# Relative position bias: the table's high and low halves multiplied in one pass of 64 stationary columns and added after the read-back

## The chip, the cores and the metric

The kernel runs on one core of one Trainium2 chip. The metric is the device time of one execution in microseconds (us), as the median of several executions. TensorE is the matrix engine (PE in the rows, PEld for its weight loads), VectorE is DVE, ScalarE is ACT, GpSimd is POOL and SyncE is SP. ACTq and SPq are the instruction queues of ACT and SP where they issue DMAs.

## The reference

Two transformer blocks over 256 rows of width 2048, in float32. The first has retention, a block attention and a feed-forward layer. The second has a memory attention (C), a sparse attention with a learned index (A) and a latent attention (B), then gates and an output product. Only attention A reads the part that is changed, the relative position bias:

```python
def t5_bucket(dist):                       # 32 buckets
    n = jnp.maximum(dist, 0)
    large = 16 + (jnp.log(max(n,1) / 16) / math.log(128 / 16) * 16).astype(int32)
    return jnp.where(n < 16, n, jnp.minimum(large, 31))

# in dsa_attention, for a block of 128 queries:
score = einsum('bths,bth->bts', relu(q_idx . k_idx), w_idx) * IDX_SCALE   # causal
sel   = top_k(score, 64)
logits = (q . k[sel]) * A_SCALE
bias   = rel_table[t5_bucket(pos_q - pos[sel])]       # rel_table is (32, 8 heads)
p      = softmax(where(valid, logits + bias, -inf))
```

So for each of 8 heads, 256 queries and up to 256 keys, one entry of a 32 by 8 table is added to a logit.

## The kernel before, in words

**The stream.** All weights lie in memory as 842 groups of 128 partitions by 1024 floats (512 KB), in the order of use. SP loads one group at a time into a ring of four buffers (RAW). ACT copies a group to WH, rounded to the matrix engine's float32 form (the high half, L931). DVE writes WL = RAW - WH (the low half, L1379). TensorE takes the group in 12 matmuls of 512 columns (L600 to L602: high by high, high by low, low by high). The ring ties them: the load of group g+4 waits for DVE's split of group g, and ACT's split of group g+4 waits until TensorE has used group g. A product of 512 output columns is 8 groups. Each engine runs its own program in a fixed order written out by hand; between the splits, at fixed steps p of a phase, it does the small work of the attentions.

**The bias, first part (phase gates_ret, 32 groups).** At six steps of each of two loop turns (BIAS_AT), 12 times in all: POOL writes distances DI for 8 queries of each of the four groups of 32 partitions, against 128 keys (L506); DVE turns them into a one-hot OH, 128 partitions (4 query groups by 32 buckets) by 1024 columns (L1556, L1557); TensorE multiplies with the table (L744). REL holds the table as a high and a low half, each 128 by 32 (8 heads for each of the four query groups, block by block). For each of two PSUM banks it runs two passes that sum in the same 32 output rows: high half times one-hot, low half times one-hot. ACT copies the 32 rows to BE (L1105) and stores them to bias_scratch in memory (L1107), where a row is a pair of query group and head.

**The bias, second part.** After phase a_proj ACT issues four DMAs (L1252) that read bias_scratch back with queries on the partitions, one DMA for each 32 partitions, into BIAS (128 by 8 heads by 384). They stand in ACT's program behind the last evacuation of a_proj and ahead of everything of phase b_proj. DVE waits for them at step 3 of gates_b0 (L1779) and adds the selection mask to BIAS in two halves (L1781). The heads of attention A read BIAS at L1424.

**Phase b_proj (24 groups)**, which follows the four issues, holds the index scores. At step 0 TensorE transposes the index keys (L869) and ACT copies them (L1261). At odd steps TensorE transposes one pair of index heads (L874) and ACT copies it to QKT (L1264), behind its split of that step. At even steps from 2 on TensorE multiplies them (L882, L883), behind a wait for ACT's copy (idx_ready), and ACT applies the relu (L1269, L1270). DVE sums at odd steps (L1755), and selects from step 18 on.

Of the kernel before, what the change touches and what calls it, by code (L numbers as in the profile page):

```python
# [21 lines left out]
F32 = mybir.dt.float32  # L22
F32R = mybir.dt.float32r
I32 = mybir.dt.int32
ALU = mybir.AluOpType
ACT = mybir.ActivationFunctionType
# [3 lines left out]
P = 128  # L30
# [19 lines left out]
CAUS = 3 * P  # L50
BUCKETS, REL_HEADS = 32, 8
# [106 lines left out]
class Chain:  # L158
# [5 lines left out]
    def link(self, ins):  # L164

        self.k += 1
        ins.then_inc(self.sem, 1)
        self.wait(self.sem, self.total + self.k + self.i * self.per if self.per else self.total + self.k)
# [9 lines left out]
def build(nc, x_in, mem_in, w_stream, params, final_w, pos_pack, constants, out):  # L178
    with ExitStack() as ctx:
        def sem(name):  # L180
            return ctx.enter_context(nc.semaphore(name))
# [5 lines left out]
        def take(nbytes):  # L187
            at = cursor[0]
            cursor[0] += nbytes
            return at  # L190

        def sb(name, shape, dt, at):
            return nc.alloc_sbuf_tensor_at(name, shape, dt, offset=at)

        KB = 1024
        at_x, at_ht, at_pa, at_pb, at_u2 = take(16 * KB), take(32 * KB), take(36 * KB), take(16 * KB), take(16 * KB)
        at_u0, at_u1 = take(16 * KB), take(16 * KB)
# [24 lines left out]
        CKV = sb("CKV", [P, T, 2 * W], F32, at_sgx)  # L222
        JUNK = sb("JUNK", [P, T, D], F32, at_u1)
        BIAS = sb("BIAS", [P, REL_HEADS, CAUS], F32, at_u2)
        LATT = sb("LATT", [P, 6, 2, S], F32R, at_sgx + 4 * KB)

        SG = {"merge_moba": sb("SG_MOBA", [P, T, CH], F32, at_u2), "merge_c": sb("SG_C", [P, T, CH], F32, at_u2 + 12 * KB),
# [14 lines left out]

        DI = sb("DI", [P, 8, P], I32, at_x)
        OH = sb("OH", [P, 2, 8, P], F32R, at_x + 4 * KB)
        BE = sb("BE", [32, 8, P], F32, at_x + 12 * KB)
        RAW = sb("RAW", [P, RING, GK, CH], F32, take(16 * KB))
        WH = sb("WH", [P, RING, GK, CH], F32R, take(16 * KB))
        WL = sb("WL", [P, RING, GK, CH], F32R, take(16 * KB))
# [5 lines left out]
        REL = sb("REL", [P, 2, 32], F32R, take(256))  # L254
# [7 lines left out]
        assert cursor[0] <= nc.sbuf_usable_end  # L262
        PS = ctx.enter_context(nc.psum_tensor("PS", [P, 8, 512], F32))

        bias_scratch = nc.dram_tensor("bias_scratch", (32, 3, 32, P), F32, kind="Internal").ap()
        x_scratch = nc.dram_tensor("x_scratch", (S, D), F32, kind="Internal").ap()

        def con(name, rows=P):
# [72 lines left out]
        bias_copied = sem("bias_copied")  # L341
        bias_stored = sem("bias_stored")
        bias_loaded = sem("bias_loaded")
# [240 lines left out]
        def _(pe):  # L584
# [151 lines left out]
            def bias_step(i, p):  # L736
                if p not in BIAS_AT:
                    return
                k = At(BIAS_AT.index(p), i, len(BIAS_AT))
                pe.wait_ge(onehot, k.count(1))  # L740
                pe.wait_ge(bias_copied, k.count(1))
                for b in range(2):
                    for part in range(2):
                        ins = pe.matmul(PS[0:32, 4 + b, :], REL[:, part, :],  # L744
                                        OH[:, k.base % 2, 4 * b:4 * b + 4, :].rearrange("p q s -> p (q s)"), start=part == 0, stop=part == 1)
                ins.then_inc(bias_done, 1)
            pe.wait_ge(rel_lo, 1)
            product_loop("gates_ret", 2, [(GD, HT)] * 2, bias_step)
# [92 lines left out]
            with pe.Fori(0, FB - 1) as b:  # L841
                g = At(g0 + 2 * GD, b, 3 * GD)
# [59 lines left out]
            for c in range(3):  # L902
                product(At(g0), At(n0 + c), 2 * c, 2, LATT)
            for c in range(4):
                product(At(g0), At(n0 + 3 + c), 6 + c, 1, LATT[:, 4:6])

# [15 lines left out]
        def _(act):  # L922
            ch = Chain(act.wait_ge, act_chain)
            link = ch.link
# [100 lines left out]
            for t in range(T):  # L1025
                act.wait_ge(x_first[t], 16)
                ins = act.activation(PS[:, 4 * t:4 * t + 4, :].rearrange("p b n -> p (b n)"), X[:, t, :], ACT.Square,
                                     scale=D ** -0.5, accum_out=MS[:, t:t + 1])
# [9 lines left out]
            g = At(GROUP0["moba_proj"])  # L1038
# [10 lines left out]
            for a in range(2):  # L1049
                act.activation(ROPE[:, 1, a], ANG[:, 0], ACT.Sin)  # L1050
                ins = act.activation(ROPE[:, 0, a], ANG[:, 1], ACT.Sin, scale=-1.0, bias=con("hpi"))
# [46 lines left out]
            def bias_step(i, p):  # L1098
                if p not in BIAS_AT:
                    return  # L1100
                s = BIAS_AT.index(p)
                k = At(s, i, len(BIAS_AT))
                act.wait_ge(bias_done, k.count(3))
                act.wait_ge(bias_stored, k.count(1) * 16)
                act.activation(BE[:].rearrange("p (b q) s -> p b (q s)", b=2), PS[0:32, 4:6, :], ACT.Copy).then_inc(bias_copied, 1)  # L1105
                act.wait_ge(bias_copied, k.count(2))
                act.dma_start(bias_scratch[:, s % 3, ds(i * 16 + s // 3 * 8, 8), :], BE[:]).then_inc(bias_stored, 16)  # L1107

# [5 lines left out]
            for p in range(NCH * GW):  # L1114
# [7 lines left out]
                if p == 3:  # L1122
                    act.wait_ge(mem_loaded, 16)
                    for t in range(T):
                        ins = act.activation(JUNK[:, t, :], MEMR[:, t, :], ACT.Square, scale=D ** -0.5, accum_out=MS[:, t:t + 1])
# [21 lines left out]
            for p in range(GD):  # L1147
                g = At(GROUP0["mem0"])
# [37 lines left out]
            with act.Fori(0, FB - 1) as b:  # L1186
                g = At(g0 + 2 * GD, b, 3 * GD)
# [9 lines left out]
            for p in range(GD):  # L1197
                g = At(GROUP0["mem1"])
# [8 lines left out]
            for p in range(2 * GD):  # L1207
                g = At(GROUP0["mem2"])
# [4 lines left out]
                if p in (4, 5):  # L1213
                    act.wait_ge(x_done, p - 2)
                    ins = act.activation(PS[:, 4:8, :].rearrange("p b n -> p (b n)"), X[:, p - 4, :], ACT.Square,
                                         scale=D ** -0.5, accum_out=MST[:, 0, 0, p - 4:p - 3])
# [20 lines left out]
            with act.Fori(0, 4) as i:  # L1237
                ch.enter(i, 3)
                g = At(GROUP0["a_proj"], i, 2 * GD)
                for p in range(2 * GD):  # L1240
                    split(g, p + RING)
                    if p % GD == GD - 1:
                        c = p // GD
                        dst = PAC[:, ds(i * 2 + c, 1)].rearrange("p a t n -> p (a t) n")
# [3 lines left out]

            act.wait_ge(head_out, C0 + 4 + 1)
            act.wait_ge(bias_stored, 16 * (NBIAS + 1))  # L1250
            for g in range(4):
                act.dma_start(BIAS[32 * g:32 * g + 32, :, :].rearrange("p h (s k) -> p h s k", s=3),  # L1252
                              bias_scratch[8 * g:8 * g + 8].rearrange("h s p k -> p h s k")).then_inc(bias_loaded, 16)

            squares = [(PAC[:, h // 4, t, h % 4 * P:(h % 4 + 1) * P], MST[:, 0, t, h:h + 1]) for h in range(8) for t in range(T)]
            squares += [(PAC[:, 2, t, h * P:(h + 1) * P], MST[:, 1, t, h:h + 1]) for h in range(2) for t in range(T)]
# [20 lines left out]
            for p in range(3 * GD):  # L1277
                g = At(GROUP0["b_proj"])
# [13 lines left out]
            def latent_squares(p):  # L1292
# [11 lines left out]
                elif 4 <= p < 7:  # L1304
                    transposed("lat", LATT, [2 * p - 8, 2 * p - 7], "lat")
            gates_b("gates_b0", 0, 1, latent_squares)
# [64 lines left out]
        def _(dve):  # L1371
            ch = Chain(dve.wait_ge, dve_chain)
            link = ch.link
# [41 lines left out]
            def head_scores(br, H, M, h):  # L1415
# [6 lines left out]
                if br["causal"]:  # L1422
                    mask = BIAS[:, ds(h, 1), :].rearrange("p a n -> p (a n)") if br is ASP else con("mask")
                    link(dve.scalar_tensor_tensor(out=SC[:, 0:CAUS], in0=PS[:, 6, 0:CAUS], scalar=br["scale"], in1=mask,  # L1424
# [155 lines left out]
            for p in range(NCH * GW):  # L1580
# [4 lines left out]
                if p in (8, 12):  # L1585
                    dve.wait_ge(norm_rstd, 2)
                    ins = scaled_rows(MEMR, MEMR, p // 4 - 2)
# [82 lines left out]
            with dve.Fori(0, FB - 1) as b:  # L1670
                ch.enter(b, 2 * 2 * FT)
                g = At(g0 + 2 * GD, b, 3 * GD)
# [74 lines left out]
            for p in range(3 * GD):  # L1747
                split(At(GROUP0["b_proj"]), p + RING)
                if p % 2 and 3 <= p < TOPK_AT:
                    k = (p - 3) // 2  # L1750
                    dve.wait_ge(idx_relu, k + 2)
                    for j, src in enumerate((SC, PR)):
                        for t, cols in halves:
                            w = PAC[:, 7, t, IW + 2 * k + j:IW + 2 * k + j + 1]
                            ins = dve.scalar_tensor_tensor(out=PT[:, cols], in0=src[:, cols], scalar=w, in1=PT[:, cols],  # L1755
                                                           op0=ALU.mult, op1=ALU.add)
                        link(ins)
                    dve.sem_inc(idx_sum, 1)
                if p >= TOPK_AT:
                    topk_round(p - TOPK_AT)  # L1760
            for p in range(GD):
                split(At(GROUP0["gates_b0"]), p + RING)
                if p < 2:
                    topk_round(3 * GD - TOPK_AT + p)
                if p == 2:

                    link(dve.tensor_scalar(left[:, 0:CAUS], left[:, 0:CAUS], TAKEN, -1.0, ALU.is_equal, ALU.add))
                    link(dve.scalar_tensor_tensor(out=SC[:, 0:CAUS], in0=left[:, 0:CAUS], scalar=-NEG, in1=con("mask"),
                                                  op0=ALU.mult, op1=ALU.add))

                    dve.wait_ge(lat_rstd, 1)
                    for t in range(T):
                        dve.tensor_scalar(PB[:, t, 0:512], PB[:, t, 0:512], MS[:, t:t + 1], None, ALU.mult)
                        dve.tensor_scalar(PB[:, t, PB_KV], PAC[:, 7, t, KV_LAT], MS[:, 2 + t:3 + t], None, ALU.mult)
                    dve.tensor_copy(PB[:, :, PB_KPE], PAC[:, 7, :, KPE]).then_inc(lat_rows, 1)
                if 4 <= p < 7:
                    transposed("lat", LATT, [2 * p - 8, 2 * p - 7], "lat")
                if p in (3, 4):
                    dve.wait_ge(bias_loaded, 64)  # L1779
                    half = BIAS[:, (p - 3) * 4:(p - 2) * 4]  # L1780
                    dve.tensor_tensor(half, half, SC[:, 0:CAUS].unsqueeze(1).broadcast_to([P, REL_HEADS // 2, CAUS]),  # L1781
                                      ALU.add).then_inc(sel_ready, 1)
# [166 lines left out]
```

## Time and profile before

| | before |
|---|---|
| median of 3 runs | 2513.46 us (2513.05, 2513.46, 2515.88) |
| span of the profiled execution | 2513.8 us |
| PE busy | 2480.8 us, 99% |
| DVE busy | 1502.5 us, 60% |
| ACT busy | 1232.3 us, 49% |
| POOL busy | 233.7 us, 9% |
| mean granted TensorE clock | 0.998 |
| DMA | 461.07 MB, 130129 packets |

The page gives the profiled execution's span and no further time of it; the median of the runs lies 0.34 us under that span. Busy times of matmuls overlap: a matmul of 512 columns is written with 0.39 us, while the next one starts 0.23 us after it. What one costs is the distance between two starts.

### The profile page before, as it was taken

Reading aid. Unit: us, or ns where it says so; the run is one execution under the profiler, and the core shown is the slowest. Engines: PE = TensorE matmul, PEld = TensorE weight load, DVE = VectorE, ACT = ScalarE, POOL = GpSimd, SP = SyncE. Lnnn points to the kernel's source line nnn. Section 1 sums busy time; section 2 is a strip of 40 time slices with the busy share of each in tenths; the row PEclk is TensorE's granted clock in tenths of the full one; section 3 lists DMA queues with packets and bytes.
Section 4 is the critical chain, followed back from the end, with each engine's and each line's share of the span. In section 5 each row is a group of like instructions: output and inputs, shape, how many; then the busy total and the mean of one; then the engine's idle time right before and its main releaser. Section 6 shows DMA issues by size and latency. Waiting matters only on the chain.

```text
span 2513.8 us, 35958 instructions
## 1 busy us (share of the span) xinstructions
PE 2480.8 (99%) x11882; PEld 2054.1 (82%) x11882; DVE 1502.5 (60%) x1799; ACT 1232.3 (49%) x1632; POOL 233.7 (9%) x277
## 2 busy tenths in 40 slices
PE   7999999999999999999999999999999999999999
PEld 6888878877888888888888888888877788777887
DVE  4444445486656777777777776444446655554564
ACT  4444545544445444444444445454547555555443
POOL 0011224231000000000000000010100100432000
PEclk9999999999999999999999999999999999999999
DMA  6555545565655555555555556555564545444654
GB/s 235 192 186 169 173 162 171 171 216 194 210 185 176 187 188 190 186 188 188 189 187 190 186 189 211 194 186 171 170 193 160 173 156 183 164 152 149 226 184 159
DMA packets 130129, 461.07 MB, mean 183 GB/s; under 512 B 14224, under 2 KB 17552, under 8 KB 129168
## 3 DMA queue, kind: packets, MB, share of 16 engines
q1 hardware_dynamic: 121536, 443.60, 52.9%
q10 hardware_dynamic: 8528, 16.58, 2.0%
q8 instruction: 43, 0.70, 0.1%
q14 instruction: 22, 0.18, 0.0%
HBM read 454.36 MB, written 5.77 MB: 183 GB/s over the span
## 4 chain that ended last, share of the span: by engine, by line
PE 95%; DVE 1%; POOL 1%; ACT 1%; issue 1%; DMA 0%; ACTq 0%; POOLq 0%; SPq 0%; DVEq 0%
PE PS L600 20%; PE PS L602 20%; PE PS L601 20%; PE PS L800 13%; PE PS L802 7%; PE PS L824 3%; PE PS L826 3%; PE PS L825 3%; PE PS L681 1%; PE PS L698 1%; PE PS L661 1%; PE PS L641 1%; DVE WL L1379 1%; ACT WH L931 0%; PE PS L744 0%
## 5 line engine op out<-in xcount | busy, mean ns | idle before, releaser
L1379 DVE TENSOR_TENSOR WL<-RAW,WH 128x1024 fp32r<-128x1024 f32 x842 | 1056.2, 1256 | 952.8 <-ACT WH L931 948.3
L931 ACT ACTIVATE WH<-RAW 128x1024 fp32r<-128x1024 f32 x842 | 890.4, 1060 | 1158.6 <-PE PS L602 764.3
L600 PE MATMUL PS<-WH,HT 128*128 128x512 f32 x1824 | 730.4, 400 | 3.0 <-DVE HT L1408 1.2
L602 PE MATMUL PS<-WH,HT 128*128 128x512 f32 x1824 | 712.9, 391 | 0.0
L601 PE MATMUL PS<-WL,HT 128*128 128x512 f32 x1824 | 711.7, 390 | 0.0
L800 PE MATMUL PS<-HT,WH 128*128 128x512 f32 x1408 | 498.2, 399 | 0.0
L600 PEld LDWEIGHTS PS<-WH,HT 128*128 128x128 f32 x1824 | 343.4, 188 | 78.7 <-issue 9.1
L602 PEld LDWEIGHTS PS<-WH,HT 128*128 128x128 f32 x1824 | 343.0, 188 | 73.8
L601 PEld LDWEIGHTS PS<-WL,HT 128*128 128x128 f32 x1824 | 343.7, 188 | 67.3
L802 PE MATMUL PS<-HT,WL 128*128 128x256 f32 x1408 | 395.4, 281 | 0.0
L800 PEld LDWEIGHTS PS<-HT,WH 128*128 128x128 f32 x1408 | 264.6, 188 | 65.7
L802 PEld LDWEIGHTS PS<-HT,WL 128*128 128x128 f32 x1408 | 266.0, 189 | 0.4
L824 PE MATMUL PS<-WH,ACTT 128*128 128x512 f32 x352 | 137.2, 390 | 0.0
L826 PE MATMUL PS<-WH,ACTT 128*128 128x512 f32 x352 | 137.1, 389 | 0.0
L825 PE MATMUL PS<-WL,ACTT 128*128 128x512 f32 x352 | 137.0, 389 | 0.0
L600 PE MATMUL PS<-WH,U 128*128 128x512 f32 x320 | 130.3, 407 | 2.1 <-issue 2.1
L602 PE MATMUL PS<-WH,U 128*128 128x512 f32 x320 | 125.8, 393 | 0.0
L601 PE MATMUL PS<-WL,U 128*128 128x512 f32 x320 | 125.5, 392 | 0.0
L437 POOL TENSOR_TENSOR MS<-MS,CONST 128x2 f32<-128x2 f32 (+1 forms) x8 | 1.6, 198 | 1073.1 <-ACT PS L963 785.1
L826 PEld LDWEIGHTS PS<-WH,ACTT 128*128 128x128 f32 x352 | 66.1, 188 | 14.1
L824 PEld LDWEIGHTS PS<-WH,ACTT 128*128 128x128 f32 x352 | 66.1, 188 | 13.8
L825 PEld LDWEIGHTS PS<-WL,ACTT 128*128 128x128 f32 x352 | 66.1, 188 | 13.5
(235 smaller groups left out, 1915.1 us busy)
## 6 DMA issues: line engine op xcount, KB each, us to landing
RAW<-w_stream SPq DMA_DIRECT2D x842, 512.0 KB, 3.3
X<-x_in SPq DMA_DIRECT2D x2, 1024.0 KB, 6.7
MEMR<-mem_in ACTq DMA_DIRECT2D x1, 2048.0 KB, 11.5
X<-x_in ACTq DMA_DIRECT2D x4, 512.0 KB, 4.2
x_scratch<-X ACTq DMA_DIRECT2D x4, 512.0 KB, 3.8
X<-x_scratch ACTq DMA_DIRECT2D x1, 2048.0 KB, 9.8
out<-X ACTq DMA_DIRECT2D x4, 512.0 KB, 3.5
bias_scratch<-BE ACTq DMA_DIRECT2D x12, 128.0 KB, 2.5
```

The costliest lines, as they stand in the source:

```text
L600: pe.matmul(o, hi, WH[:, slot, kk, :], start=k == 0, stop=False)
L601: pe.matmul(o, hi, WL[:, slot, kk, :], start=False, stop=False)
L602: ins = pe.matmul(o, lo, WH[:, slot, kk, :], start=False, stop=k == nq * GK - 1)
L641: ins = pe.transpose(PS[:, 4 + at % 4, t * P:(t + 1) * P], src[:, t, k * P:(k + 1) * P], ident)
L661: ins = pe.transpose(PS[0:n, 4 + a, c * S + t * P:c * S + (t + 1) * P], QK[:, a, t, c * P:c * P + n], ident)
L800: pe.matmul(PS[:, half + f, :], WH[:, slot, kk, f * P:(f + 1) * P], HT[:, k, :, :], start=k == 0, stop=False, skip_group_check=True)
L802: ins = pe.matmul(PS[:, half + f, 0:S], WL[:, slot, kk, f * P:(f + 1) * P], HT[:, k, 0, :], start=False, stop=k == KT - 1, skip_group_chec ...
L824: pe.matmul(o, hi, WH[:, slot, kk, :], start=k == 0, stop=False)
L825: pe.matmul(o, hi, WL[:, slot, kk, :], start=False, stop=False)
L826: ins = pe.matmul(o, lo, WH[:, slot, kk, :], start=False, stop=k == FT - 1)
L931: act.activation(WH[:, g.slot(j)], RAW[:, g.slot(j)], ACT.Copy).then_inc(hi_split, 1)
L1379: dve.tensor_tensor(WL[:, s], RAW[:, s], WH[:, s].bitcast(F32), ALU.subtract).then_inc(lo_split, 1)
```

## The change

REL is taken as 64 stationary columns (32 of the high half, 32 of the low half), so one pass for each bank gives 64 output rows: the high products and the low products apart. BE, its copy and its store have 64 rows, and bias_scratch has 64. Eight DMAs in place of four read it back, four into BIAS and four into BIASL, and DVE adds the two in halves at steps 10 and 12 of b_proj. The wait for the loads moves from gates_b0 to there.

```diff
+        BIASL = sb("BIASL", [P, REL_HEADS, CAUS], F32, at_u1)
-        BE = sb("BE", [32, 8, P], F32, at_x + 12 * KB)
+        BE = sb("BE", [64, 8, P], F32, at_x + 12 * KB)
-        bias_scratch = nc.dram_tensor("bias_scratch", (32, 3, 32, P), F32, kind="Internal").ap()
+        bias_scratch = nc.dram_tensor("bias_scratch", (64, 3, 32, P), F32, kind="Internal").ap()
...
                 for b in range(2):
-                    for part in range(2):
-                        ins = pe.matmul(PS[0:32, 4 + b, :], REL[:, part, :],
-                                        OH[:, k.base % 2, 4 * b:4 * b + 4, :].rearrange("p q s -> p (q s)"), start=part == 0, stop=part == 1)
+                    ins = pe.matmul(PS[0:64, 4 + b, :], REL[:].rearrange("p a n -> p (a n)"),
+                                    OH[:, k.base % 2, 4 * b:4 * b + 4, :].rearrange("p q s -> p (q s)"), start=True, stop=True)
                 ins.then_inc(bias_done, 1)
...
-                act.activation(BE[:].rearrange("p (b q) s -> p b (q s)", b=2), PS[0:32, 4:6, :], ACT.Copy).then_inc(bias_copied, 1)
+                act.activation(BE[:].rearrange("p (b q) s -> p b (q s)", b=2), PS[0:64, 4:6, :], ACT.Copy).then_inc(bias_copied, 1)
...
             act.wait_ge(bias_stored, 16 * (NBIAS + 1))
-            for g in range(4):
-                act.dma_start(BIAS[32 * g:32 * g + 32, :, :].rearrange("p h (s k) -> p h s k", s=3),
-                              bias_scratch[8 * g:8 * g + 8].rearrange("h s p k -> p h s k")).then_inc(bias_loaded, 16)
+            for part, dst in enumerate((BIAS, BIASL)):
+                for g in range(4):
+                    h = 32 * part + 8 * g
+                    act.dma_start(dst[32 * g:32 * g + 32, :, :].rearrange("p h (s k) -> p h s k", s=3),
+                                  bias_scratch[h:h + 8].rearrange("h s p k -> p h s k")).then_inc(bias_loaded, 16)
...
+                if p in (10, 12):
+                    dve.wait_ge(bias_loaded, 128)
+                    half = slice((p - 10) * 2, (p - 10) * 2 + 4)
+                    link(dve.tensor_tensor(BIAS[:, half], BIAS[:, half], BIASL[:, half], ALU.add))
...
                 if p in (3, 4):
-                    dve.wait_ge(bias_loaded, 64)
```

## Rows read from the trace of the kernel before

**Rows 1.** The page: busy time of each engine, chain that ended last.
```profile
PE 2480.8 (99%) x11882; PEld 2054.1 (82%) x11882; DVE 1502.5 (60%) x1799; ACT 1232.3 (49%) x1632; POOL 233.7 (9%) x277
...
PE 95%; DVE 1%; POOL 1%; ACT 1%; issue 1%; DMA 0%; ACTq 0%; POOLq 0%; SPq 0%; DVEq 0%
```

**Rows 2.** Timeline of PE, first bias step: start, length, engine, line, tiles.
```profile
508.79 1.08 PE L744 MATMUL PS<-OH,REL 128*32 128x512 f32 x4
509.71 0.40 PE L600 MATMUL PS<-WH,HT 128*128 128x512 f32 x1
509.94 0.39 PE L601 MATMUL PS<-WL,HT 128*128 128x512 f32 x1
```

**Rows 3.** Instructions of L744 and tile BE: min/median/max ns, first and last start.
```profile
L744 PEld LDWEIGHTS PS<-OH,REL x48: 106/108/109, 508.6 to 598.5; 128*32 128x32 f32 x48
...
L1105 ACT ACTIVATE BE<-PS x12: 995/1016/1019, 510.0 to 600.1; 32x1024 f32<-32x1024 f32 x12
```

**Rows 4.** Timeline of ACT and its queue, end of a_proj and start of b_proj.
```profile
1858.96 0.93 ACTq L1252 DMA_DIRECT2D BIAS<-bias_scratch  x2
...
1859.92 2.79 ACTq L1252 DMA_DIRECT2D BIAS<-bias_scratch  x2
1862.84 1.06 ACT L931 ACTIVATE WH<-RAW 128x1024 fp32r<-128x1024 f32 x1 [2.21 <-issue]
1863.80 0.36 ACT L1261 ACTIVATE QKT<-PS 128x256 f32<-128x256 f32 x1
1864.99 1.06 ACT L931 ACTIVATE WH<-RAW 128x1024 fp32r<-128x1024 f32 x1 [0.82 <-PE PS L602]
1865.96 0.36 ACT L1264 ACTIVATE QKT<-PS 128x256 f32<-128x256 f32 x1
```

**Rows 5.** L1252, issues 3 and 4 one by one, with time to landing.
```profile
L1252 ACTq DMA_DIRECT2D BIAS<-bias_scratch x1: 1044/1044/1044, 1859.9 to 1859.9; - x1
...
DMA to landing us min/median/max: 9.4/9.4/9.4
...
L1252 ACTq DMA_DIRECT2D BIAS<-bias_scratch x1: 1720/1720/1720, 1861.0 to 1861.0; - x1
...
DMA to landing us min/median/max: 11.8/11.8/11.8
```

**Rows 6.** DMA queues (q1 SP, q10 ACT), stretches 1857:1861, 1861:1865, 1865:1869: packets, MB, share.
```profile
q1 hardware_dynamic: 227, 0.80, 55.2%
q10 hardware_dynamic: 109, 0.06, 4.8%
...
q10 hardware_dynamic: 1713, 0.86, 105.3%
q1 hardware_dynamic: 1, 0.00, 0.4%
...
q10 hardware_dynamic: 773, 0.39, 55.6%
```

**Rows 7.** Timeline of PE around the first product of index scores, b_proj step 2.
```profile
1867.47 0.39 PE L602 MATMUL PS<-WH,HT 128*128 128x512 f32 x1
1867.79 0.50 PE L882 MATMUL PS<-QKT 64*128 64x128 f32 x4
```

**Rows 8.** Timeline of DVE, split of step 15 of b_proj; below it L1781.
```profile
1913.59 1.23 DVE L1379 TENSOR_TENSOR WL<-RAW,WH 128x1024 fp32r<-128x1024 f32 x1 [2.60 <-ACT WH L931]
...
L1781 DVE TENSOR_TENSOR BIAS<-BIAS,SC x2: 1749/1750/1751, 1952.6 to 1956.2; 128x1536 f32<-128x1536 f32 x2
```

**Rows 9.** PE after its first long wait (timeline); stretch 18:21 by windows (third from last: clock).
```profile
14.28 1.94 PE L641 MATMUL PS<-CONST,ROWS 128*128 128x128 f32 x8 [14.28 <-DVE ROWS L1391]
17.43 0.79 PE L600 MATMUL PS<-WH,HT 128*128 128x512 f32 x1 [1.21 <-DVE HT L1408]
...
21.34 0.40 PE L600 MATMUL PS<-WH,HT 128*128 128x512 f32 x1
...
18.00:21.00 3.00, 3.00 (x8) 2.31 (x7) 3.00 (x4) 1.56 (x2) 0.00 (x0) 1.00 0.57 198
```

## The prediction

> **What bounds the kernel now.** I read the page first. PE is busy for 99% of the span and carries 95% of the chain that ended last; DVE and ACT stand at 60% and 49% [rows 1]. So an instruction taken off PE is worth its full distance to the next one, and a microsecond that PE has to wait costs a microsecond. Work put on DVE, ACT or a queue costs nothing until it makes PE wait. Hence I went to the two places that the change touches and read there how late the thing is that PE waits for: the timeline of PE at a bias step [rows 2], and the timelines of ACT, its queue and PE at the start of b_proj, where the read-back is issued [rows 4, 7], with the packets of the DMA queues beside them [rows 6].
>
> **Removed: 24 matmuls.** In a bias step four matmuls of 512 columns take 508.79 to 509.71 us, 0.92 us, or 0.23 us each, the same as the 0.23 us between two matmuls of the weight stream with 128 stationary columns, at 509.71 and 509.94 [rows 2]. Since 32 and 128 columns cost the same, 64 will. The load of the columns takes 0.108 us for 32 [rows 3] and fits under the 0.23 us. There are 48 such matmuls [rows 3]; 24 go: 24 x 0.23 = 5.5 us off PE, with nothing behind them that was late. It can't be more by much, and not less unless 64 columns were slower than 128.
>
> **Copy and store.** The copy takes 1.016 us on 32 partitions [rows 3]; ACT's split of 1024 elements on 128 partitions takes 1.06 us [rows 4], so 64 rows add nothing. The store is 256 KB in place of 128 KB. Nothing needs it before the next bias step's copy; ACT has only the wait for it there. Bounds: 0 to a us or two of waiting for ACT, which a ring of four groups hides. I take 0.
>
> **The four further issues.** This is the cost, and I work it out in full, because the issues stand in ACT's program in front of its splits and copies of b_proj. The four issues before took 0.93 us for two and 2.79 us for two; ACT stood still 2.21 us for them and went on at 1862.84, 0.13 us after the last issue ended at 1862.71 [rows 4]. The third took 1.044 us and the fourth 1.720 [rows 5], so they grow: half of 0.93, 1.04, 1.72. That is not the price of an instruction but of a queue that fills. One DMA is 384 KB in runs of 512 bytes, 768 packets. The third issue ended near 1860.96, with 2304 packets issued and at most 109 moved [rows 5, 6]: 2200 pending. The fourth ended at 1862.71; 109 + 1.71 us x 428 a us (1713 in 4 us) = 841 moved of 3072 [rows 6]: 2230 pending. Both agree: an issue ends when some 2200 packets are left pending. Eight DMAs are 6144 packets, so the eighth issue ends when 3944 have moved. By 1865, 1822 have. From 1865 to 1869 the stream's loads share the engines: 773 was measured [rows 6], with two loads there; with one load of 128 packets (1.24 us of the engines, by the 227 packets that held 55.2% of them for 4 us [rows 6]) it is up to (4 - 1.24) x 428 = 1180. I take the middle, 980. That leaves 1144 packets, 2.7 us alone: **the last issue ends near 1871.7, 9.0 us later than before.**
>
> What waits behind it: ACT's split, its copy of the keys, the next split, its copy L1264. Before, these ran with a pause of 0.82 us for PE [rows 4]; back to back they end 2.8 us after the last issue, and with a hand-over of 0.2 us TensorE's L882 can start 3.0 us after it. It started at 1867.79, straight behind its matmul of 1867.47 [rows 7], so before there was 2.1 us of slack. After: 1871.7 + 3.0 = 1874.7, which is **6.9 us of PE standing idle**. The rest of the ring is no later: the groups of steps 1 to 3 are split already, and step 4's split is done before PE gets there.
>
> **After a stand-still the matmuls are slow for a while.** At the start of the kernel, after 14.28 us without matmuls, eight transposes and 1.21 us more of waiting, the products start at 17.43, and the tenth at 21.34 [rows 9]: nine distances in 3.9 us, where nine of 0.23 are 2.1 us. That is 1.8 us lost. The granted clock is written 1.00 there, the 2.4 GHz level, though the mean distance of 0.43 us is nearly twice the usual; I go by the distance. The other waits of PE are far shorter than 7 us, so the trace shows only what 14 us does. Bounds 0 to 1.8 us; I take 1.8, because nothing at all would run on PE for 6.9 us.
>
> The Trainium skill, "TensorE: Matmul & The Clock Gate", Part 1, says that the throttled state is the default and activity releases it; after an idle gap matmuls start at the half rate again. The start of this trace agrees. By that rule the 1.8 us is due here too; without it the sum is 1.8 us lower.
>
> **Weight loads.** A stream load issued in the BIAS traffic moved one packet in 4 us [rows 6]. In the changed kernel the traffic lasts longer, but ACT's own stand-still also holds back the next loads (they wait for the splits), and when they start about 1100 packets of BIAS are left, as before, where PE started L882 straight behind the stream [rows 7]. I take 0; bound up to 2 us.
>
> **The two additions.** 128 x 1536 on DVE: L1781 of the same size takes 1.75 us [rows 8]. Behind the split of an even step DVE stands idle for 2.60 us, as until 1913.59 [rows 8]; the addition fits. The fourth load landed 11.8 us after its issue [rows 5], so the eighth lands by some 1871.7 + 12 = 1884. Steps 2 to 15 lie between 1867.79 and 1913.59 [rows 7, 8], 3.5 us each, so step 10 comes near 1896, and the stall shifts it further: the wait is met. The wait removed at gates_b0 was long met. 0 us; if the cover were gone, two times 1.75 us of DVE, inside a ring four groups deep.
>
> **Sum:** -5.5 + 6.9 + 1.8 = +3.2 us. On the profiled span 2513.8 that is 2517.0; on the median, 0.34 us under the span, 2516.7. What tells from no change in this kernel is about 0.2%, 5.0 us; this is 0.13%.
>
> **Rivals.**
> (a) *The issues stay short and PE never waits.* Four times the mean of the first two, 0.47 us [rows 4], are 1.9 us, within the 2.1 us of slack (1867.79 - 1862.71 - 3.0). Then 2513.46 - 5.5 = 2508.0, faster by 0.22%. Against it: the fourth issue took 1.72 us [rows 5], over three times that.
> The Trainium skill, "DMA: Bandwidth & Descriptors", section "Issuing engines are not separate DMA queues", says the sequencer's time to initiate a DMA is usually small beside the DMA itself. By it (a) holds. The rows disagree for this access pattern: 1.72 us for the fourth.
> (b) *The growth stops at 1.72 us.* Four times 1.72 is 6.9 us of delay, the stall 4.8 us, no slow matmuls: 2513.46 - 5.5 + 4.8 = 2512.8, not slower. For it: only four points of the growth are seen.
> (c) *Slower: each further issue lasts as long as landings are apart at the end.* Issue 3 landed at 1869.3 and issue 4 at 1872.8, 3.5 us apart [rows 5]. Then the delay is 14.0 us, the stall 11.9 us, plus 1.8: 2513.46 - 5.5 + 11.9 + 1.8 = 2521.7, slower by 0.33%. It holds if the mixed rate of 773 packets in 4 us [rows 6] persists although the stream pauses; it is over 0.2% slower from a delay of some 11 us on.
> (d) *The passes aren't halved in time* (64 columns cost two passes): then +5.5 on my sum, 2522.2. The 128-column rows at 0.23 us speak against it; 2 in 100.
>
> **How the numbers follow.** My forecast 0.52 (own range 2514.3 to 2519), (a) 0.13, (b) 0.13, (c) and (d) 0.22. Faster by over 0.2% is (a) less what misses the bound: 0.12. Slower by over 0.2% (above 2518.5) is (c), (d) and the top of my own case: 0.27. The rest 0.61. The range runs from (a) at 2508.0 to just under (c), 2521.0.
>
> **What would show it.** L744: 24 matmuls, 0.46 us from the first to the next L600. L1252: eight issues, the last ending 8 to 10 us later against the first than before, and ACT's idle time "issue" near 11 us. PE: a wait of about 7 us before L882 at step 2 of b_proj, released by ACT's L1264, and spacings of 0.43 us behind it. DVE: two additions of 1.8 us without a wait. Wrong if PE has no such wait, if it is over 10 us, or if PE waits elsewhere in b_proj for late weights.

## The result: 6.6 us slower

| | before | after |
|---|---|---|
| median of 7 runs | 2515.88 us | 2522.48 us |
| lowest to highest | 2513.05 to 2516.61 | 2520.21 to 2524.24 |
| span of the profiled execution | 2513.8 us | 2520.3 us |
| mean granted clock | 0.998 | 0.997 |

The ratio of the runs is 1.0027, 95% interval 1.0018 to 1.0037: slower, and clear of no change. I had forecast +3.2 us on 2513.46 and a range up to 2521.0. The measured time lies outside it, partly because the kernel before itself came out 2.4 us higher over seven runs than over the first three: two of the first three lay at 2513, and the other five of the seven between 2515.66 and 2516.61. The 0.34 us of which I made a rule (the median of the runs lies under the span) compared two different executions. The device time of the kernel before is 1.74 to 1.94 us over the span of the same execution wherever both are listed, so the profiled execution, with its span of 2513.8, is one of the higher group, and 2513.46 is a median of the lower one. For the changed kernel the distance is about 2.2 us. The difference of the spans, 6.5 us, is what the profiles explain. One of the eleven executions of before_late_copy_wait (below) took 3539.27 us at a mean granted clock of 0.656; it is counted in the median given there, 2512.88, which is 2512.62 without it. Line numbers of the changed kernel differ a little (L600 to L602 became L601 to L603, L1252 became L1254).

**Bias stage.** The timeline of PE in the changed kernel, the first bias step, the seventh and the twelfth (answers to [rows 2]) with the wait behind it, then the instructions of L744 and of the copy and store of BE (to [rows 3]):

```profile
508.93 0.62 PE L744 MATMUL PS<-OH,REL 128*64 128x512 f32 x2
...
555.97 0.67 PE L744 MATMUL PS<-OH,REL 128*64 128x512 f32 x2 [0.19 <-DVE OH L1559]
...
594.27 0.63 PE L744 MATMUL PS<-OH,REL 128*64 128x512 f32 x2
597.44 0.47 PE L601 MATMUL PS<-WH,U 128*128 128x512 f32 x1 [2.54 <-issue]
```
```profile
L744 PEld LDWEIGHTS PS<-OH,REL x24: 132/134/137, 508.8 to 594.3; 128*64 128x64 f32 x24
...
L1105 ACT ACTIVATE BE<-PS x12: 997/1003/1011, 510.1 to 596.3; 64x1024 f32<-64x1024 f32 x12
...
L1107 ACTq DMA_DIRECT2D bias_scratch<-BE x12: 481/482/571, 511.3 to 597.5; - x12
```

Half the matmuls are gone, as forecast. From the first to the twelfth start of L744 it was 89.29 us (508.79 to 598.08) and is 85.34: 3.95 us less, where eleven times 0.46 would be 5.06. New is PE waiting for the one-hot (L1559). Behind the twelfth step PE waits at the end of the stage, 2.54 us here. In the kernel before it did so too, 2.07 us, which I had not read. The rows name no releaser; before_late_copy_wait, below, shows that it is the wait for the last copy of BE:

```profile
601.24 0.56 PE L600 MATMUL PS<-WH,U 128*128 128x512 f32 x1 [2.07 <-issue]
```

**Start of b_proj.** The timeline of ACT and its queue in the changed kernel (answers to [rows 4]), then the single issues 5 to 8 into BIASL (to [rows 5]):

```profile
1855.15 0.93 ACTq L1254 DMA_DIRECT2D BIAS<-bias_scratch  x2
1855.81 1.01 ACT L936 ACTIVATE PAC<-PS 128x1024 f32 x1
1856.12 2.74 ACTq L1254 DMA_DIRECT2D BIAS<-bias_scratch  x2
1858.88 10.47 ACTq L1254 DMA_DIRECT2D BIASL<-bias_scratch  x4
1869.48 1.06 ACT L931 ACTIVATE WH<-RAW 128x1024 fp32r<-128x1024 f32 x1 [12.66 <-issue]
...
1871.65 0.38 ACT L1266 ACTIVATE QKT<-PS 128x256 f32<-128x256 f32 x1
```
```profile
L1254 ACTq DMA_DIRECT2D BIASL<-bias_scratch x1: 1743/1743/1743, 1858.9 to 1858.9; - x1
...
L1254 ACTq DMA_DIRECT2D BIASL<-bias_scratch x1: 2614/2614/2614, 1860.7 to 1860.7; - x1
...
L1254 ACTq DMA_DIRECT2D BIASL<-bias_scratch x1: 4192/4192/4192, 1863.3 to 1863.3; - x1
...
L1254 ACTq DMA_DIRECT2D BIASL<-bias_scratch x1: 1836/1836/1836, 1867.5 to 1867.5; - x1
```

The issues grow to 4.19 us; the eighth takes 1.84. ACT stands still for 12.66 us in place of 2.21. PE in the same place (answers to [rows 7]), then PE's granted clock by windows (columns: stretch, length, busy time of PE, PEld, DVE, ACT, POOL, granted clock, DMA share, GB/s):

```profile
1863.68 0.39 PE L603 MATMUL PS<-WH,HT 128*128 128x512 f32 x1
1872.08 0.81 PE L882 MATMUL PS<-QKT 64*128 64x128 f32 x4 [8.01 <-ACT QKT L1266]
...
1874.26 0.63 PE L602 MATMUL PS<-WL,HT 128*128 128x512 f32 x1
1874.68 0.63 PE L603 MATMUL PS<-WH,HT 128*128 128x512 f32 x1
```
```profile
1866.00:1868.00 2.00, 0.00 (x0) 0.00 (x0) 0.00 (x0) 0.00 (x0) 0.00 (x0) 1.00 1.21 188
1868.00:1870.00 2.00, 0.00 (x0) 0.00 (x0) 0.00 (x0) 0.52 (x1) 0.00 (x0) 0.60 1.22 212
1870.00:1872.00 2.00, 0.00 (x0) 0.00 (x0) 1.34 (x2) 2.00 (x5) 0.00 (x0) 0.50 1.21 211
1872.00:1874.00 2.00, 1.92 (x9) 1.27 (x10) 2.00 (x2) 1.18 (x3) 0.00 (x0) 0.50 1.28 220
...
1875.00:1877.00 2.00, 2.00 (x9) 1.57 (x9) 0.00 (x0) 0.00 (x0) 0.00 (x0) 0.95 1.03 339
```

PE waits 8.01 us for ACT's copy; in the middle of the wait the granted clock falls to 0.50, 1.2 GHz, and it stays there for the first 2 to 3 us of work, with 0.42 us between matmuls. Of the forecast's steps this is the one that was right in kind, place and releaser.

**Where the 6.5 us are,** by the starts of the same instructions in both kernels:

| stretch | shift after it | change (+ is slower) |
|---|---|---|
| up to the first L744 (508.79, 508.93) | +0.1 | +0.1 |
| first to twelfth L744 | -3.8 | -3.9 |
| twelfth L744 to first matmul of up_ret (601.24, 597.44) | -3.8 | 0.0 |
| up to L882 at step 2 of b_proj (1867.79, 1872.08) | +4.3 | +8.1 |
| L882 at step 2 to step 4 (1874.58, 1880.31), slow matmuls | +5.7 | +1.4 |
| gates_b0, behind a PE wait of 2.48 us | +6.7 | +0.9 |

The fourth and fifth lines are the stall, 9.5 us in all. The last line was not in my sum, and the second was there with another size. All of it is of one profiled execution of each kernel.

### The profile page after: what moved, and what is told of

It reads as the page before. It is cut to its first block, busy times and chain, and to the rows that moved or that the text cites. A ratio compares the mean times of both kernels' runs of the same rounds, so it can differ in the third digit from the quotient of the medians.

```text
span 2520.3 us, 35918 instructions
## 1 busy us (share of the span) xinstructions
PE 2479.1 (98%) x11858; PEld 2054.2 (82%) x11858; DVE 1509.6 (60%) x1801; ACT 1232.4 (49%) x1632; POOL 234.0 (9%) x277
## 4 chain that ended last, share of the span: by engine, by line
PE 94%; ACT 1%; DVE 1%; POOL 1%; issue 1%; ACTq 1%; DMA 0%; POOLq 0%; SPq 0%; DVEq 0%
PE PS L601 20%; PE PS L603 20%; PE PS L602 20%; PE PS L800 13%; PE PS L802 7%; PE PS L824 3%; PE PS L826 3%; PE PS L825 3%; PE PS L682 1%; PE PS L699 1%; PE PS L642 1%; PE PS L662 1%; ACT WH L931 1%; ACTq L1254 1%; DVE WL L1381 0%
## 5 line engine op out<-in xcount | busy, mean ns | idle before, releaser
L601 PE MATMUL PS<-WH,HT 128*128 128x512 f32 x1824 | 731.3, 401 | 2.3 <-DVE HT L1410 1.2
L603 PE MATMUL PS<-WH,HT 128*128 128x512 f32 x1824 | 713.8, 391 | 0.0
L602 PE MATMUL PS<-WL,HT 128*128 128x512 f32 x1824 | 712.7, 391 | 0.0
L601 PEld LDWEIGHTS PS<-WH,HT 128*128 128x128 f32 x1824 | 344.3, 189 | 78.3 <-issue 8.2
L603 PEld LDWEIGHTS PS<-WH,HT 128*128 128x128 f32 x1824 | 343.5, 188 | 73.9
L602 PEld LDWEIGHTS PS<-WL,HT 128*128 128x128 f32 x1824 | 344.5, 189 | 67.3
L601 PE MATMUL PS<-WH,U 128*128 128x512 f32 x320 | 130.4, 408 | 2.5 <-issue 2.5
L603 PE MATMUL PS<-WH,U 128*128 128x512 f32 x320 | 125.8, 393 | 0.0
L602 PE MATMUL PS<-WL,U 128*128 128x512 f32 x320 | 125.3, 392 | 0.0
```

Of the source, the lines that this page charges most:

```text
L601: pe.matmul(o, hi, WH[:, slot, kk, :], start=k == 0, stop=False)
L602: pe.matmul(o, hi, WL[:, slot, kk, :], start=False, stop=False)
L603: ins = pe.matmul(o, lo, WH[:, slot, kk, :], start=False, stop=k == nq * GK - 1)
```

## The experiments

Medians are of the label's runs beside runs of the kernel before on the same chip; ratios are with their 95% interval. Each expectation stands as it was written ahead of the run.

### Loads alone: x4_loads

```diff
 for g in range(4): act.dma_start(BIAS[32 * g: ...], bias_scratch[8 * g:8 * g + 8] ...)
+for g in range(4): act.dma_start(BIASL[32 * g: ...], bias_scratch[8 * g:8 * g + 8] ...)
...
-                    dve.wait_ge(bias_loaded, 64)
+                    dve.wait_ge(bias_loaded, 128)
```

> The kernel before (two passes, 32 rows) with nothing but four further loads issued behind the four, into BIASL, from the same 32 rows; BIASL isn't used. Theory I (the issues of a full queue hold ACT, and with it PE): a PE wait of 8.0 us before the first product of index scores and slow matmuls behind it, 1.4 us, so 9.4 us above before, with perhaps 1 us more or less at the wait of 2.5 us in gates_b0. Rival R1 (the slowdown comes from the 64-row copy and store or from the additions on DVE): 0 to 1 us above before, no PE wait there.

Measured: 2526.27 us against 2515.84, +10.4, ratio 1.0043 (1.0029 to 1.0057), 1 us more than expected, with a shorter wait of PE (6.68 us, expected 8.0). The timeline of PE in x4_loads:

```profile
1874.90 0.80 PE L883 MATMUL PS<-QKT 64*128 64x128 f32 x4 [6.68 <-ACT QKT L1268]
```

The issues took 12.9 us from the first's start to the last's end (1859.30 to 1872.18), so the loads alone, with neither one pass nor additions, bring the whole slowdown and more. R1 falls. Besides the slow matmuls at 602 us that the kernel before has too, the profile has two such stretches behind waits, at 1876 and 1961; the second is the further 1 us that the expectation allowed for.

### The rest alone: halves_four_loads

```diff
-            for part, dst in enumerate((BIAS, BIASL)):   # eight loads
+            for g in range(4):                            # four, as before
...
-                    link(dve.tensor_tensor(BIAS[:, half], BIAS[:, half], BIASL[:, half], ALU.add))
```

> The changed kernel without its four loads into BIASL and without the two additions (the low half of the table is left out of the result); one pass, 64 rows copied and stored as in the change. Theory I: 3.8 us below before, no wait at b_proj. Rival R1: still above before, by 3 to 6 us.

Measured: 2511.58 against 2515.84, -4.3, ratio 0.9984 (0.9974 to 0.9993). With x4_loads the two parts add to +6.2, and the change measured +6.6. The change is a gain of 4 us and a loss of 10.

### Where the gain of the one pass stops: halves_half_store

The edit is against halves_four_loads; bias_scratch has 32 rows again too.

```diff
-        BE = sb("BE", [64, 8, P], F32, at_x + 12 * KB)
+        BE = sb("BE", [32, 8, P], F32, at_x + 12 * KB)
...
-                act.activation(BE[...], PS[0:64, 4:6, :], ACT.Copy)
+                act.activation(BE[...], PS[0:32, 4:6, :], ACT.Copy)
...
```

> As the kernel with four loads and 64 rows stored, but only the 32 rows of the high half are copied and stored (the low half is left out). Theory S (the longer issue and landing of the 256 KB store hold ACT, so that DVE's one-hot is late for PE): PE has no wait before L744, the stage gains 1.1 us more, 4.9 us below before. Rival S2 (PE runs ahead of DVE, which is what bounds the close pairs of steps): the same two steps lose 0.3 us each, 3.8 us below before.

Measured: 2510.49 against 2515.84, ratio 0.9980 (0.9971 to 0.9989); 1.1 us under halves_four_loads, just the number of theory S. But the trace says that most of it isn't that. From the first to the twelfth L744 it is 84.93 us here and 85.24 there: the store is worth 0.3 us (the four kernels that share the change's bias stage lie between 85.24 and 85.38), and the one-hot is still late: PE's own 0.2 us of waiting before L744 is gone, but not that of its weight loads (1.4 us in three places, against 2.1 in five). The rest is a stretch of slow matmuls near 600 us which this kernel's profile doesn't have. By windows, first the kernel before, then halves_half_store, behind the same wait of PE at the end of the bias stage:

```profile
599.00:601.00 2.00, 0.17 (x1) 0.00 (x0) 1.23 (x1) 2.00 (x3) 0.00 (x0) 1.00 0.56 213
601.00:603.00 2.00, 1.76 (x5) 1.41 (x6) 0.00 (x0) 0.14 (x1) 0.00 (x0) 0.62 0.69 203
603.00:605.00 2.00, 2.00 (x7) 1.57 (x6) 0.00 (x0) 0.00 (x0) 0.00 (x0) 0.53 0.47 182
```
```profile
597.00:599.00 2.00, 1.43 (x6) 1.24 (x7) 0.00 (x0) 0.47 (x1) 0.00 (x0) 1.00 0.85 254
599.00:601.00 2.00, 2.00 (x10) 1.65 (x9) 0.00 (x0) 0.35 (x1) 0.00 (x0) 1.00 0.56 209
```

Both waited (2.07 and 2.53 us); one was given 1.2 GHz for some 3 us behind it, the other not. Neither S nor S2 is settled by the median, which would have misled.

### The same loads, one at a time: spread

```diff
-            for part, dst in enumerate((BIAS, BIASL)): ...      # eight issues ahead of b_proj
...
                 index_step(p)
+                if p < 8:
+                    bias_load(p)       # one of the eight, behind step p's work
```

> The changed kernel with its eight loads issued one each at the ends of steps 0 to 7 of b_proj, behind ACT's index work of the step, in place of eight in a row ahead of it. Theory I: each issue lasts under 0.6 us, no PE wait at b_proj, 3.8 us below before; 1 us either way by the wait in gates_b0. Rival R2 (the DMA traffic itself, 6144 packets, makes the weights late wherever it stands): PE waits for WL in b_proj, time near or above before.

Measured: 2511.84 against 2515.84, -4.0, ratio 0.9986 (0.9977 to 0.9995). Same instructions, same bytes and packets as the change, 10.6 us less. The tile BIASL in spread:

```profile
L1254 ACTq DMA_DIRECT2D BIASL<-bias_scratch x4: 318/318/318, 1871.6 to 1881.3; - x4
...
DMA to landing us min/median/max: 9.6/12.8/15.0
```

An issue is 0.32 us when the queue has room. Landings are late (up to 15.0 us), DVE's first addition waits 3.12 us for the last, and PE waits for none of it. R2 falls.

### Two loads more: x2_loads

```diff
+for g in range(2): act.dma_start(BIASL[32 * g: ...], bias_scratch[8 * g:8 * g + 8] ...)
```

> The kernel before with two further loads behind the four (into BIASL, not used). Theory I with a queue that holds some 2100 packets: the sixth issue ends 8.2 us after the first one starts, as in the changed kernel, so PE waits about 2.1 us before the first product of index scores; 2.1 to 4 us above before, by whether the pause is followed by slow matmuls. Rival R3 (a delay in proportion to the loads, half of x4_loads): 5 us above before, a PE wait of 3.4 us.

Measured: 2518.76 against 2516.04, +2.7, ratio 1.0011 (1.0002 to 1.0020), but between 2514.25 and 2521.93 over eleven runs. The timeline of ACT's queue and of PE in x2_loads:

```profile
1862.13 5.79 ACTq L1256 DMA_DIRECT2D BIASL<-bias_scratch  x2
```
```profile
1870.64 0.50 PE L883 MATMUL PS<-QKT 64*128 64x128 f32 x4 [2.53 <-ACT QKT L1268]
```

The sixth issue ended 8.7 us after the first began (1859.19 to 1867.92), and PE waited 2.53 us, near the 8.2 and 2.1 of the queue with a fixed room; R3 asked for 3.4 us of wait. By the packets of the stretches some 2360 of the 4608 had moved when the sixth issue ended, 2250 left, and in x4_loads 4040 of 6144 when the eighth did, 2100 left. In the profile slow matmuls follow this wait (8 of them) and the one in gates_b0 (8). The wide spread of the times suggests that it isn't so in every run, and the mean granted clock that is listed for each execution goes with it: 1.000 at 2514.25 us, 0.999 at 2516.58, 0.997 or 0.998 at all the others.

### Packets or bytes: long_runs

```diff
-        bias_scratch = nc.dram_tensor("bias_scratch", (64, 3, 32, P), ...)
+        bias_scratch = nc.dram_tensor("bias_scratch", (64, 32, 3, P), ...)
...
-  act.dma_start(dst[...].rearrange("p h (s k) -> p h s k", s=3), bias_scratch[h:h + 8].rearrange("h s p k -> p h s k"))
+  act.dma_start(dst[...], bias_scratch[h:h + 8].rearrange("h p s k -> p h (s k)"))
```

> The changed kernel with bias_scratch laid out so that one read of 1536 bytes takes the place of three of 512; eight loads in a row as in the change, same bytes. The store is then in runs of 512 bytes. Theory I-packets: 256 packets a load, 2048 in all, so no issue is held up, each under 0.6 us, no PE wait at b_proj; about 4 us below before, less up to 2 us if the store's 512 short runs hold ACT. Rival I-bytes (the queue fills by bytes): issues grow to 2 us and more, PE waits near 7 us, above before.

Measured: 2513.04 against 2516.04, -3.0, ratio 0.9989 (0.9980 to 0.9998). Eight issues in a row, the same 3.1 MB. ACT's queue in long_runs, the sixth issue alone, then q10 from 1857 to 1861, packets and MB:

```profile
1857.77 3.10 ACTq L1254 DMA_DIRECT2D BIASL<-bias_scratch  x4
1860.99 1.06 ACT L931 ACTIVATE WH<-RAW 128x1024 fp32r<-128x1024 f32 x1 [3.59 <-issue]
```
```profile
L1254 ACTq DMA_DIRECT2D BIASL<-bias_scratch x1: 1485/1485/1485, 1858.3 to 1858.3; - x1
```
```profile
q10 hardware_dynamic: 518, 0.76, 83.3%
```

0.76 MB in 518 packets is 1.5 KB each, a third as many packets. All eight issues take 5.1 us, and PE has no wait at b_proj beyond the 0.37 us at its start that the kernel before has too. Some 2.4 MB were pending when the last issue ended, where the room of the short packets was 1.1 MB: the room is counted in packets, and bytes fall as a cause. Not all came as expected: the issues take 0.36 to 0.62 us, but the sixth 1.49 us, with at most 1536 packets issued. The room of some 2200 doesn't explain that one, and it stays open. The price is in the store: its issue takes 0.63 us in place of 0.48, and the bias stage 85.77 us from the first to the twelfth L744 in place of 85.34.

### The wait behind the bias stage: before_late_copy_wait and spread_late_copy_wait

```diff
             pe.wait_ge(head_out, RET0 + 4 + 1)
-            pe.wait_ge(bias_copied, NBIAS + 1)
...
                     if merged_tiles(p):
+                        if name == "merged1" and p == GW + 1:
+                            pe.wait_ge(bias_copied, NBIAS + 1)
                         pe.wait_ge(merged_ready, chunks_before + p // GW)
```

> The kernel before, with PE's wait for the last copy of the bias (bias_copied) moved from the start of up_ret to its first transposes, five groups later, which are the first to write the banks that the copy reads. Theory W (the PE wait of 2.1 us there is for this copy, and the seven slow matmuls behind it follow from the pause): 2.1 us + 1.4 us = 3.5 us below before, no slow matmuls at 600 us. Rival (PE waits there for weights or for something else): the wait stays, same as before.

Measured: 2512.88 against 2516.04, ratio 0.9988 (0.9978 to 0.9997), -3.2, where 3.5 was expected. The wait is gone: the timeline of PE, last bias step and what follows.

```profile
599.15 1.10 PE L744 MATMUL PS<-OH,REL 128*32 128x512 f32 x4
600.09 0.40 PE L600 MATMUL PS<-WH,U 128*128 128x512 f32 x1
```

No slow matmuls follow at 600 us, but five do in gates_b0, which the kernel before did not have there.

> The spread kernel with the wait for the last copy moved in the same way. Theories I and W together: 4.0 us (spread) + 2.5 us (the wait) + 1.4 us (the slow matmuls), 8 us below before. If the last saving of the one pass is kept only when the wait is gone, this is where it shows: the gain over spread is over the 3.5 us of the kernel before with the wait moved.

Measured: 2508.89 against 2516.04, -7.2, ratio 0.9971 (0.9960 to 0.9983). 8 us was expected. Against spread it is 3.2 us less, no more than the wait was worth in the kernel before and under the 3.5 us that the expectation asked for; its profile too has five slow matmuls in gates_b0 that spread's doesn't have. Whether the last 0.46 us of the one pass is kept can't be told from this.

### The one-hot a group earlier: onehot_early

```diff
-                if p + 2 not in BIAS_AT:
+                ahead = (0, 1, 4, 7, 9, 12)
+                if p not in ahead:
                     return
-                k = At(BIAS_AT.index(p + 2), i, len(BIAS_AT))
+                k = At(ahead.index(p), i, len(BIAS_AT))
```

> The spread kernel with the late wait for the copy, and DVE's one-hot for five of the six steps of a turn made one group earlier (steps 0, 1, 4, 7, 9, 12 in place of 0, 2, 5, 8, 10, 13). Theory S2 (what is left of the loss in the bias stage comes from DVE making the one-hot just in time, now that PE is quicker): from the first to the twelfth start of L744 84.2 to 84.6 us in place of 85.3, no wait of PE on OH, and 0.7 to 1 us below spread_late_copy_wait, 8 us below before. Rival (DVE then has to wait for POOL's distances and its splits come late): the stage no shorter, same or slower than spread_late_copy_wait.

Measured: 2508.22 against 2515.92, -7.7, ratio 0.9969 (0.9957 to 0.9982); 0.7 us under spread_late_copy_wait, but by medians taken on two chips, each with a spread of 1 to 2 us. The trace is plainer: from the first to the twelfth L744 (509.33 to 593.79) it is 84.46 us, against 85.38 in spread_late_copy_wait, and one wait is left, where none was expected:

```profile
556.02 0.68 PE L744 MATMUL PS<-OH,REL 128*64 128x512 f32 x2 [0.19 <-DVE OH L1563]
```

So S2 holds for most of the loss. This is the fastest version of the study.

## Why the prediction was wrong, step by step

By the spans the change cost 6.5 us where I had 3.2. The 3.3 us between them are the removed matmuls (1.6 short of their gain), the further issues (1.2 more), the slow matmuls behind the stall (0.4 less) and a term that I had left out (0.9). The step that failed first is the gain of the removed matmuls.

**The removed matmuls, -5.5 us: mis-sized, -3.9 measured.** The price of one, 0.23 us, was right, and 64 columns cost no more than 32. What failed is the claim "with nothing behind them that was late". Two things were just in time. DVE's one-hot is made two groups ahead, and once PE is quicker it waits for it, mostly between the sixth and the eighth step (0.7 us of the 1.1 us lost; onehot_early gives 0.9 back). And the last step's 0.46 us ran into PE's wait for the copy of BE, which grew from 2.07 to 2.54 us. I had read PE at one bias step, not the end of the stage; that wait stood in the trace. The store, which I took at 0, costs 0.3 to 0.4 us, in part the same loss, since it too comes as a later one-hot: its issue is 0.48 us in place of 0.32, and 0.63 in long_runs goes with 85.77 us.

**The further issues, +6.9 us: mechanism right, size low; +8.1 measured.** The queue with room for some 2200 packets stands: the eighth issue ended at 1869.35, when by the packets of the stretches some 4100 of the 6144 had moved, 2040 left. What was low is the delay, 9.0 us against 10.45 (14.20 from the first issue's start to the last one's end, 3.75 before). The packets moved at other rates than I took. By 4 us stretches from 1857 on, q10 in the changed kernel:

```profile
q10 hardware_dynamic: 1607, 0.81, 103.1%
...
q10 hardware_dynamic: 821, 0.41, 63.5%
q1 hardware_dynamic: 124, 0.47, 50.5%
...
q10 hardware_dynamic: 1406, 0.71, 114.1%
```

Beside one load of 512 KB, 821 moved; I had taken 980, between 773 and 1180, on the thought that half the stream traffic leaves more room. It was nearly the rate beside two loads. Alone, 1406 and 1607 moved in 4 us, not 1713. ACT's chain behind it took 2.7 us (1869.35 to 1872.08), where I had 3.0.

**Slow matmuls behind the stall, +1.8 us: +1.4 measured,** and now with a granted clock of 0.50 beside it. In x4_loads the stall was 6.68 us and the same followed.

The Trainium skill, "TensorE: Matmul & The Clock Gate", Part 1, calls the throttled state the default and activity what lifts it. The rows agree: the granted clock is 0.50 at the end of the wait and shortly after, and 0.95 from 1875 to 1877.

**Left out: waits of 2 to 3 us, +0.9 us.** I wrote that the trace "shows only what 14 us does". It didn't: behind a wait of 2.07 us the kernel before ran seven matmuls at 0.43 us, granted clock 0.53 to 0.62 (the windows above), and I had not looked there. Nor had I looked at this wait of 3.30 us:

```profile
365.78 1.85 PE L661 MATMUL PS<-CONST,QK 128*128 128x128 f32 x8 [3.30 <-POOL QK L488]
...
367.85 0.63 PE L601 MATMUL PS<-WL,HT 128*128 128x512 f32 x1
368.28 0.63 PE L602 MATMUL PS<-WH,HT 128*128 128x512 f32 x1
```

The granted clock is 0.50 from 367 to 369, and slow matmuls follow this wait in all eleven profiles. In gates_b0 both kernels wait 2.48 us. The windows there, kernel before, then the changed one:

```profile
1951.00:1953.00 2.00, 1.42 (x8) 1.25 (x9) 2.00 (x5) 0.84 (x2) 0.57 (x1) 1.00 0.33 131
```
```profile
1957.00:1959.00 2.00, 1.69 (x6) 1.58 (x7) 2.00 (x4) 0.90 (x2) 0.30 (x1) 0.53 0.33 123
```

Same wait, same releaser, and only one is slowed: 1.5 us lost, 0.5 of it won back in a shorter wait some groups on (0.90 to 0.35 us). Over the eleven kernels profiled here, this wait of 2.47 to 2.49 us was followed by slow matmuls in six (the changed kernel, x4_loads, x2_loads, both late_copy_wait, onehot_early) and not in five. What decides it is open. It isn't the length of the wait; the kernels differ in the time at which the wait comes. Nor need it be the kernel: PE's program is the same in all eleven up to the first L744, and yet behind the wait of 14 us 7 to 12 matmuls are written with 0.6 us or more, behind the one of 3.3 us 4 to 8, and the first L744 starts between 508.64 and 509.86 us. So a part of this differs from one execution to the next, and the 0.9 us is what two executions showed, not yet a price of the change.

**The additions, the weight loads, the copy: 0, right.** Here is DVE in the changed kernel, an addition in its place between splits (answers to [rows 8]):

```profile
1903.07 1.75 DVE L1764 TENSOR_TENSOR BIAS<-BIAS,BIASL 128x1536 f32<-128x1536 f32 x1
1905.82 1.23 DVE L1381 TENSOR_TENSOR WL<-RAW,WH 128x1024 fp32r<-128x1024 f32 x1 [1.00 <-ACT WH L931]
```

**The rivals.** (a) and (b) fell with the issues of 1.74 to 4.19 us, and here too the rows disagree with what (a) took from the Trainium skill, "DMA: Bandwidth & Descriptors", section "Issuing engines are not separate DMA queues": where the queue is full, the sixth and the seventh issue took 2.61 and 4.19 us, longer than the 1.8 us in which 768 packets move alone. (c) came nearest with 2521.7 us, but by luck: its condition, that the mixed rate of 773 packets in 4 us persists, held for one stretch only (821, then 1406), the delay was 10.45 us and not 14.0, and its gain was too large and its starting time 2.4 us too low. (d) fell: two matmuls take 0.46 us.

## What to carry to other kernels

An issue is cheap only while its queue has room. Count the packets (contiguous runs) of DMAs in a row on one queue, and where they pass what the queue holds, put the issues between other work, or make the runs longer: here that turned a loss of 6.6 us into a gain of 3 to 4 us. When work is taken off the bounding engine, look at every wait behind it in the stage, the end of the stage included, for how early its releaser is; a saving stops at the first that was just in time. And a wait of the matrix engine may cost more than its length. And where the runs fall in two groups, as those of the kernel before did, the median of three was 2.4 us under that of seven.

## What the runs showed of the hardware that I had not expected

- The queue of ACT held some 2000 to 2250 packets of 512 bytes, in four kernels; the next issue then took as long as the packets in front needed, up to 4.19 us for one of 0.32.
- With packets of 1.5 KB in place of 0.5 KB, eight issues of the same bytes took 5.1 us in place of 14.2; one of them took 1.49 us, which is open.
- The issue itself grew with the packets of one DMA: stores of 128 KB and 256 KB in runs of 4 KB 0.32 and 0.48 us, 256 KB in runs of 512 bytes 0.63 us.
- The granted clock fell to 0.50 (1.2 GHz) behind waits of PE as short as 2.07 us, and did not behind others of 2.48 and 2.53 us; each time some 3 us of work at half the rate, 1 to 1.6 us lost. A median that differs by 1 us between such kernels says nothing of their code until the windows have been read, and one profile shows one execution: x2_loads ran between 2514.25 us (mean granted clock 1.000) and 2521.93 (0.997).
